# Attention units scaled one step behind their sums, products two units ahead, and more modulation chunks among them

## The chip, the cores and the metric

The kernel runs on one core of a Trainium2 chip. The metric is the device time of one execution in microseconds, as the median of several runs. A core has five engines with instruction streams of their own: TensorE (PE, with its weight loads as PEld), VectorE (DVE), ScalarE (ACT), GpSimd (POOL) and SyncE (SP), which here only issues DMAs. They are ordered by semaphores alone.

## The reference, cut to what matters

One step of a small model with two layers. The first layer mixes 384 tokens (128 of a prompt, 256 of a grid, so three tiles of 128) by attention, the second by a Hyena operator (a long convolution by FFT). Each is followed by a mixture of 32 experts.

```
m = silu(c) @ ada_w[l] + ada_b[l]             # 6 x 1024 values per layer: shifts, scales, gates
h = rmsnorm(x) * (1 + sc1) + sh1
p = h @ w_in                                   # q latent, kv latent, rotary key, nq, nk, nv
q = rmsnorm(rmsnorm(q_lat) @ w_q_up)           # 8 MLA heads of 96
k, v = from rmsnorm(kv_lat) @ w_kv_up          # keys normalised, too
nq, nk = rmsnorm per head                      # 8 neighbourhood heads of 64
out = softmax(q k^T * s (+ bias, mask)) v @ w_out
x = x + g1 * out
x = x + g2 * moe(rmsnorm(x) * (1 + sc2) + sh2)
```

The product of `silu(c)` with `ada_w` is the modulation: per layer 1024 x 6144 weights, 24 MB. It depends on nothing but `c`, so it can be computed anywhere before its use.

## The kernel before

The program is written engine by engine, each with its order of work by hand. Signals (`sig(name)`) count events; `.by(ins, i)` sets event i, `.at(eng, i)` waits for it. `link` makes an engine wait for its own last instruction.

**Modulation chunks.** The modulation is cut into 24 chunks of 512 columns (2 MB each, `ada`, 72 matmul instructions). Four of layer 0 come first; the other 20 (`chunks`) are spread over the attention: chunk 0 and 1 at units 7 and 9 (`at_unit`), the rest at 18 of the 24 pairs (`at_pair`). VectorE copies each result (`ada_row`, line 964). SyncE writes finished rows to DRAM in groups (`store_mod`, line 1867) and reads back the first layer's gate, broadcast to all partitions (`load_gate`, line 1879), as soon as the rows of chunk 1 have landed: a wait on SyncE's queue.

**The ring.** Weights come into a ring of three slots. Item n lies in slot n % 3 and may be loaded when item n - 3 is used: items 0 to 3 are chunks, 4 to 7 the columns of `w_in` (latents, nq, nk, nv), 8 the two up projections ("up"), 9 to 28 the 20 chunks, 29 and 30 the output weights, later ones belong to the Hyena layer. SyncE issues them in this order, so one that waits holds all behind it. "up" is free after the last k product.

**Units.** There are 13 units (`units`): nq, nk and q for three tiles each, k for four (the fourth is the cached context). For a unit TensorE makes the product (`produce`), ScalarE squares it (`square_unit`, one buffer `sq`), VectorE sums the squares per head (line 1032, for k also 1035), GpSimd raises to the power -0.5 (`unit_power`, line 1723), VectorE scales by that, by the gain, and rotates q and k of tiles 1 and 2 (line 952 is the helper of all these), TensorE turns the unit (`turn_unit`, lines 542, 544) and ScalarE copies it out. TensorE's loop makes the product of unit n+1, then a chunk if there is one, then turns unit n. The three nv products and the turned latents (`turn_latents`) stand before the product of unit 6. Scaled units lie in two buffers, and each accumulation takes the next of eight PSUM banks in turn (`open_`).

**Pairs.** Then 24 pairs of heads (12 MLA, 12 neighbourhood; the first four of each dozen have one block of 128 keys, the other eight three). For pair i TensorE makes the scores, turns the probabilities of pair i-2, multiplies those of pair i-3 with the values, and does a chunk if there is one, in bank 7. VectorE takes the maximum (line 1092), ScalarE the exponential (line 1540).

**Masks.** The bias of the neighbourhood heads is loaded (line 1914) after the "up" weights and masked on GpSimd (lines 1797, 1800) between the powers of units 5 and 6.

Of the kernel before, what the change touches and what calls it, by code (L numbers as in the profile page):

```python
# [171 lines left out]
def build(nc, a, stage=99):  # L172
    ctx = ExitStack()
    with ctx:
# [73 lines left out]

        def item(n, *dims):
            return v(RING + (n % 3) * MSLOT, *dims)  # L250
# [40 lines left out]
        for n, k in enumerate(items):  # L291
            loads[n % 3] += 16 * ndma.get(k[0], 1)
            landed[k] = loads[n % 3]
# [51 lines left out]
        at_unit = {7: chunks[0], 9: chunks[1]}  # L345
        at_pair = {int(1.32 * n) + 1: c for n, c in enumerate(chunks[2:])}
# [57 lines left out]
        w3_slot = RING + (number[("w3",)] % 3) * MSLOT  # L404
        W3, skip_row = v(w3_slot, 2 * D), v(w3_slot + 2 * D, 2 * D)
        nrow = [v(RING + (number["hyout", g] % 3) * MSLOT + 4096, 512) for g in range(2)]
# [18 lines left out]
        def _(pe):  # L425
# [3 lines left out]
            def arrived(k):  # L429
                pe.wait_ge(item_loaded[number[k] % 3], landed[k])  # L430
                return number[k]
# [5 lines left out]
            def ada(l, n, bank=None):  # L437
                i = arrived(("ada", l, n))
                w = item(i, KC, 512)
                brow = v(RING + (i % 3) * MSLOT + 4096, 512)  # L440
# [51 lines left out]
            def attention():  # L492
# [3 lines left out]
                for t in range(T):  # L496
                    hT_ready(0, t)
                    for kind, c0, c1 in (("qlat", 0, QR), ("kvr", QR, WIN0)):
                        o = open_(pe, kind, t, [("lat", t)])
# [4 lines left out]
                def produce(kind, t):  # L504
                    if kind in ("nq", "nk", "nv"):
                        w = item(arrived(("win", {"nq": 1, "nk": 2, "nv": 3}[kind])), KC, 512)
                        i = proj[kind, t, 0]
                        o = open_(pe, "proj", i, [("nv", t)] if kind == "nv" else [("normed", units.index((kind, t)))])
# [4 lines left out]
                    base = RING + (arrived(("up",)) % 3) * MSLOT  # L513
                    wq, wkv = v(base, 3, NH * QK), v(base + 2304, NH * 2 * NOPE)
                    sig("latT").at(pe, t)
                    for j in range(2):
                        i = proj[kind, t, j]
                        n = units.index((kind, t))
                        if kind == "q":
                            o = open_(pe, "proj", i, [("normed", n)])  # L520
                            for c in range(3):
                                last = mm(o[:, 0:384], LT[:, c, t * P:(t + 1) * P], wq[:, c, j * 384:(j + 1) * 384], c == 0, c == 2)
                        else:
                            o = open_(pe, "proj", i, [("normed", n), ("vout", t)])
# [3 lines left out]
                def turn_unit(kind, t):  # L528
# [18 lines left out]
                def turn_latents(t):  # L547
                    o = open_(pe, "latT", t, [("latT", t)])
# [399 lines left out]
        def _(dve):  # L948
# [67 lines left out]
            def attention():  # L1016
# [7 lines left out]
                for n, (kind, t) in enumerate(units):  # L1024
                    if n - 1 in at_unit:
                        l, c = at_unit[n - 1]
                        ada_row((l, c))
                    b = n % 2

                    sig("sq").at(dve, n)  # L1030
                    w = NOPE if kind != "q" else QK
# [4 lines left out]
                    sig("hms").by(red, n)  # L1036
                    sig("hrs").at(dve, n)
# [41 lines left out]
                    sig("normed").by(ins, n)  # L1079

# [345 lines left out]
        def _(act):  # L1426
# [35 lines left out]
            def attention():  # L1462
# [46 lines left out]
                square_unit(0)  # L1509
                for n, (kind, t) in enumerate(units):  # L1510
                    if n + 1 < len(units):
                        if units[n + 1] == ("q", 0):
# [7 lines left out]
                        square_unit(n + 1)  # L1520
# [196 lines left out]
        def _(pool):  # L1717
# [38 lines left out]
            def hyena():  # L1756
                for b in range(4):
# [4 lines left out]
                    if b == 0:  # L1762
                        pool.wait_ge(item_loaded[number[("w3",)] % 3], landed[("w3",)])
# [14 lines left out]
            if stage >= 1:  # L1778
# [15 lines left out]
                for hf in range(2):  # L1794
                    b = bias[64 * hf:64 * hf + 64].rearrange("p a b c d -> p (a b c) d")

                    link(pool.affine_select(out=b[:, :, 0:48], in_=b[:, :, 0:48], compare_op=ALU.is_ge, fill=NEG,
                                            base=8, pattern=[[0, 64], [1, 48]], channel_multiplier=-1))

                    sig("bias").by(pool.affine_select(out=b[:, :, 16:64], in_=b[:, :, 16:64], compare_op=ALU.is_ge, fill=NEG,  # L1800
                                                      base=-9, pattern=[[0, 64], [-1, 48]], channel_multiplier=1), hf)
                    sig("bias").at(pool, hf)
                for n in range(6, len(units)):
                    unit_power(n)
# [12 lines left out]
        def _(sp):  # L1817
            def load(k):
                n = number[k]
                if n >= 3:  # L1820
                    wait_used(sp, items[n - 3])
                s = item_loaded[n % 3]
                if k[0] == "ada":
                    _, l, c = k
                    sp.dma_start(item(n, KC, 512), a["ada_w"][l].rearrange("(p k) n -> p k n", k=KC)[:, :, c * 512:(c + 1) * 512]).then_inc(s, 16)  # L1825
                    o = RING + (n % 3) * MSLOT + 4096
# [4 lines left out]
                elif k[0] == "up":  # L1831
                    sp.dma_start(item(n, 3, NH * QK), a["mla_w_q_up"][0].rearrange("(c p) n -> p c n", p=P)).then_inc(s, 16)
                    sp.dma_start(v(RING + (n % 3) * MSLOT + 2304, NH * 2 * NOPE), a["mla_w_kv_up"][0]).then_inc(s, 16)
# [99 lines left out]
            if stage >= 3:  # L1933
# [9 lines left out]
                for k in items1[:3]:  # L1943
                    o = number[k] % 3 * MSLOT
# [74 lines left out]
```

## Time and profile before

| | us |
|---|---|
| median of 3 runs | 1339.37 (1339.36 to 1351.76) |
| the profiled execution | 1351.24 |
| its span | 1349.5 |
| TensorE busy | 1215.2 (90%) |
| VectorE, ScalarE, GpSimd busy | 589.8, 267.6, 201.0 |
| attention's units (from the first product of nq to the first scores) | 73.5 to 191 |
| attention's 24 pairs | 191 to 308.2 |

The span is from the first to the last instruction; the execution takes 1.7 us more. A busy share is an average over stages of different kinds. The chain that ended last lies 84% on TensorE and 5% on VectorE.

### The profile page before, as it was taken

The numbers are of one execution on the slowest core, as the hardware profiler recorded it, in microseconds if no ns is written. First come the engines' busy times: TensorE is split into PE (matmuls) and PEld (weight loads), VectorE is DVE, ScalarE is ACT, GpSimd is POOL, SyncE is SP. The second block draws the span as 40 slices with busy tenths as digits, with TensorE's granted clock in tenths as the row PEclk, the third lists the DMA queues.
The fourth block names the chain that finished last, engine by engine and source line by source line (L and its number), as shares of the span: only waits on it lengthen the run. The fifth ranks groups of instructions, "written<-read, shape, count | busy, mean of one in ns | idle before, by whom it ended". The sixth has DMA issues, their size and how long they took to land.

```text
span 1349.5 us, 26273 instructions
## 1 busy us (share of the span) xinstructions
PE 1215.2 (90%) x9235; PEld 704.2 (52%) x9236; DVE 589.8 (44%) x1223; ACT 267.6 (20%) x648; POOL 201.0 (15%) x249
## 2 busy tenths in 40 slices
PE   4799868989878899999979999999986899999996
PEld 3554545664545455555555654344554555555553
DVE  0122443462342344444554334777455144445445
ACT  1111332440201112112132113111010111211211
POOL 1025210000101122222200001111010022221231
PEclk9899977999778899999989999899985989999998
DMA  9533159993530989999952222000135089996894
GB/s 318 210 128 119 63 195 358 347 369 112 231 143 28 417 340 422 379 393 396 379 189 80 108 77 80 0 1 0 75 141 243 0 348 412 383 378 262 321 422 168
DMA packets 80143, 304.77 MB, mean 226 GB/s; under 512 B 10872, under 2 KB 11809, under 8 KB 54729
## 3 DMA queue, kind: packets, MB, share of 16 engines
q1 hardware_dynamic: 77098, 298.66, 57.0%
q10 hardware_dynamic: 2752, 4.53, 0.9%
q8 instruction: 51, 0.84, 0.3%
q0 software_dynamic: 224, 0.61, 0.1%
q14 instruction: 18, 0.15, 0.0%
HBM read 301.52 MB, written 2.24 MB: 225 GB/s over the span
## 4 chain that ended last, share of the span: by engine, by line
PE 84%; DVE 5%; DMA 4%; issue 2%; SPq 2%; ACT 1%; POOL 0%; POOLq 0%; DVEq 0%; ACTq 0%
PE banks L427 82%; DMA arena<-in_ada_b 3%; DVE arena L952 3%; SPq L1827 1%; PE banks L594 1%; DMA mod_rows<-arena 1%; PE banks L478 1%; SPq L1825 0%; PE banks L793 0%; DVE arena L998 0%; POOL arena L1723 0%; PE banks L542 0%; DVE arena L1092 0%; ACT arena L1459 0%; ACT arena L1550 0%
## 5 line engine op out<-in xcount | busy, mean ns | idle before, releaser
L427 PE MATMUL banks<-arena 32*128 32x256 f32 (+11 forms) x8904 | 1172.7, 424 | 88.8 <-DVE arena L952 15.6
L427 PEld LDWEIGHTS banks<-arena 128*32 128x32 f32 (+4 forms) x8904 | 662.5, 156 | 572.0 <-issue 406.5
L952 DVE TENSOR_TENSOR arena<-banks,arena 128x64 f32<-128x64 f32 (+4 forms) x284 | 113.9, 413 | 109.0 <-PE banks L427 74.5
L952 DVE TENSOR_TENSOR arena<-arena 128x384 f32<-128x384 f32 (+11 forms) x229 | 153.7, 677 | 4.9 <-PE banks L427 0.5
L1210 DVE SCALAR_TENSOR_TENSOR arena<-arena 128x768 f32<-128x768 f32 x81 | 82.9, 1024 | 92.3 <-issue 88.1
L1748 POOL COPY arena<-arena 128x256 f32 x79 | 65.0, 823 | 288.4 <-PE banks L427 154.9
L1584 ACT ACTIVATE arena<-banks 128x512 f32<-128x512 f32 x79 | 47.2, 597 | 250.8 <-PE banks L427 250.8
L1220 DVE TENSOR_SCALAR arena<-arena 128x64 f32<-128x64 f32 x79 | 15.4, 195 | 180.3 <-ACT arena L1588 180.3
L1739 POOL TENSOR_TENSOR arena<-arena 128x256 f32<-128x256 f32 x81 | 59.7, 737 | 225.3 <-PE banks L427 225.3
L1722 POOL TENSOR_SCALAR arena<-arena 128x8 f32<-128x8 f32 (+2 forms) x28 | 10.3, 369 | 379.2 <-ACT arena L1443 264.5
L1309 DVE TENSOR_SCALAR arena<-arena 128x385 f32<-128x385 f32 x24 | 11.6, 481 | 82.4 <-ACT arena L1645 82.4
L1222 DVE RECIPROCAL arena<-arena 128x64 f32<-128x64 f32 x79 | 43.7, 553 | 2.7
L1588 ACT ACTIVATE arena<-banks 128x64 f32<-128x64 f32 x79 | 17.7, 224 | 126.9 <-PE banks L427 126.9
L964 DVE COPY arena<-banks 128x128 f32<-128x128 f32 x24 | 7.0, 292 | 72.2 <-PE banks L427 72.2
L1580 ACT ACTIVATE arena<-banks 128x256 f32<-128x256 f32 x79 | 30.3, 384 | 41.3 <-PE banks L427 41.3
L1540 ACT ACTIVATE arena<-banks,arena 128x384 f32<-128x384 f32 (+1 forms) x48 | 24.0, 506 | 70.4 <-DVE arena L1093 61.3
L1443 ACT ACTIVATE arena<-arena 128x1024 f32<-128x1024 f32 x12 | 12.7, 1057 | 120.9 <-DVE arena L952 111.6
L1760 POOL TENSOR_TENSOR arena<-arena 128x512 f32<-128x512 f32 x4 | 5.1, 1263 | 209.2 <-DVE arena L952 209.2
L1723 POOL TENSOR_TENSOR arena<-arena 128x8 f32<-128x8 f32 (+2 forms) x28 | 30.5, 1090 | 2.3
L1644 ACT ACTIVATE arena<-banks,arena 128x128 f32<-128x128 f32 x24 | 8.8, 369 | 100.3 <-PE banks L427 100.3
L1195 DVE COPY arena<-banks 128x256 f32<-128x256 f32 x16 | 6.8, 425 | 48.2 <-PE banks L427 48.2
L1032 DVE TENSOR_REDUCE arena<-arena 128x8 f32<-128x512 f32 (+1 forms) x13 | 9.7, 744 | 38.4 <-ACT arena L1486 19.5
(144 smaller groups left out, 441.4 us busy)
## 6 DMA issues: line engine op xcount, KB each, us to landing
arena<-in_moe_w_gate SPq DMA_DIRECT2D x64, 1024.0 KB, 7.7
arena<-in_moe_w_up SPq DMA_DIRECT2D x64, 1024.0 KB, 9.8
arena<-in_moe_w_down SPq DMA_DIRECT2D x64, 1024.0 KB, 9.9
arena<-in_ada_w SPq DMA_DIRECT2D x24, 2048.0 KB
arena<-in_hy_w_in SPq DMA_DIRECT2D x6, 2048.0 KB
arena<-in_attn_w_in SPq DMA_DIRECT2D x3, 2048.0 KB
arena<-mod_rows SPq DMA_DIRECT2D x8, 512.0 KB, 8.8
arena<-in_attn_w_out SPq DMA_DIRECT2D x2, 2048.0 KB
```

The source lines that it names most:

```text
L427: return pe.matmul(out, lhsT, rhs, start=start, stop=stop, skip_group_check=True)
L952: return dve.tensor_tensor(o, p, q, op)
L1210: return dve.scalar_tensor_tensor(parts, posr, first_row[:, bass.ds(c, 1)], wr, ALU.is_equal, ALU.mult)
L1220: dve.tensor_scalar(e1, ex, 1.0, None, ALU.add).then_inc(s_["moe_dve"], 1)
L1222: dve.reciprocal(e2, e1).then_inc(s_["moe_dve"], 1)
L1540: ins = act.activation(PB[i % 2][:, r, 0:n, :].rearrange("p b k -> p (b k)"), ps[:, 2 * (i % 2) + r, 0:n * P], ACT.Exp, bias=negmax[:, c:c ...
L1580: act.activation(ysb, py, ACT.Copy).then_inc(s_["moe_y"], 1)
L1584: act.activation(gsb.rearrange("p i q f -> p (i q f)"), pg, ACT.Copy).then_inc(s_["moe_g"], 1)
L1588: act.activation(ex, pt[:, 0:2 * M].rearrange("p (f m) -> p f m", f=2), ACT.Exp, scale=-1.0).then_inc(s_["moe_e"], 1)
L1723: sig(name).by(pool.tensor_tensor(dst, dst, half_[:, 0:n], ALU.pow), i)
L1739: return pool.tensor_tensor(*two, bc(ones, 2), ALU.mult)
L1748: pool.tensor_copy(xcur, XS[:, :, bass.ds(first, M)]).then_inc(s_["moe_x"], 1)
```

## The change

Six edits, all around the attention:

- The ring: items 9 to 14 (chunks 0 to 5) use slots 0 and 1 in turn, and slot 2 stays with "up" until item 15. An item may be loaded when the last earlier item of its slot is used.
- Seven chunks (0 to 6) now go with units 6 to 12, the other 13 with pairs 1, 2, 4, 6, 8, 10, 12, 14, 16, 18, 20, 21 and 23.
- TensorE and ScalarE make products and squares two units ahead.
- VectorE sums the squares of unit n+1 before it scales unit n.
- PSUM banks of this phase are fixed: products in banks 0 to 5, turns in 6 and 7, chunks in 7.
- The bias is loaded before items 7 and 8, and masked on GpSimd behind the powers of units 1 and 3.

```diff
+        def place_of(n):
+            return n % 3 if n < 9 else (n - 9) % 2 if n < 15 else (n + 2) % 3
...
-        at_unit = {7: chunks[0], 9: chunks[1]}
-        at_pair = {int(1.32 * n) + 1: c for n, c in enumerate(chunks[2:])}
+        at_unit = {6 + n: c for n, c in enumerate(chunks[:7])}
+        at_pair = {int(1.9 * n) + 1: c for n, c in enumerate(chunks[7:])}
...
-                            o = open_(pe, "proj", i, [("normed", n)])
+                            o = open_(pe, "proj", i, [("normed", n)], n % 3 * 2 + j)
...
-                        o = open_(pe, "uT", i, [("uT", i)])
+                        o = open_(pe, "uT", i, [("uT", i)], 6 + j)
...
-                produce("nq", 0)
+                produce(*units[0])
+                produce(*units[1])
                 for n, (kind, t) in enumerate(units):
-                    if n + 1 < len(units):
-                        if units[n + 1] == ("q", 0):
+                    if n + 2 < len(units):
+                        if units[n + 2] == ("q", 0):
...
-                        produce(*units[n + 1])
+                        produce(*units[n + 2])
                     if n in at_unit:
-                        ada(*at_unit[n])
+                        ada(*at_unit[n], 7)
                     turn_unit(kind, t)
...
+                mean_squares(0)
+                for n, (kind, t) in enumerate(units):
+                    if n + 1 < len(units):
+                        mean_squares(n + 1)
+                    if n - 1 in at_unit:
+                        ada_row(at_unit[n - 1])
+                    b = n % 2
                     sig("hrs").at(dve, n)
...
                 square_unit(0)
+                square_unit(1)
...
-                        square_unit(n + 1)
+                        square_unit(n + 2)
                     turned(kind, t)
...
-                for n in range(6):
+                for n in range(len(units)):
                     unit_power(n)
-                pool.wait_ge(in_bias, 16)
+                    if n in (1, 3):
+                        hf = n // 2
+                        pool.wait_ge(in_bias, 16)
...
-                if n >= 3:
-                    wait_used(sp, items[n - 3])
+                held = [m for m in range(n) if place_of(m) == place_of(n)]
+                if held:
+                    wait_used(sp, items[held[-1]])
...
                 load(items0[6])
+                sp.dma_start(bias.rearrange("p a b c d -> p (a b c d)"), a["bias"]).then_inc(in_bias, 16)
                 load(items0[7])
                 load(items0[8])
-                sp.dma_start(bias.rearrange("p a b c d -> p (a b c d)"), a["bias"]).then_inc(in_bias, 16)
```

## Rows read from the trace of the kernel before

**Rows 1.** Busy time by stretch: each engine, granted clock, DMA share, GB/s.

```profile
73.50:137.00 63.50, 63.50 (x165) 29.05 (x164) 15.85 (x21) 8.15 (x21) 25.43 (x18) 1.00 0.36 131
137.00:191.00 54.00, 37.75 (x273) 24.14 (x271) 25.70 (x54) 19.58 (x43) 13.27 (x14) 0.86 0.28 100
191.00:308.20 117.20, 103.48 (x1732) 74.54 (x1733) 51.07 (x147) 44.21 (x144) 0.00 (x0) 0.90 0.96 345
```

**Rows 2.** Timeline of the q and k units: start, length, engine, line.

```profile
138.25 4.08 PE L427 MATMUL banks<-arena 128*128 128x384 f32 x12
...
148.09 1.08 PE L542 MATMUL banks<-arena 128*96 128x128 f32 x8 [1.45 <-DVE arena L952]
...
155.55 0.94 DVE L1032 TENSOR_REDUCE arena<-arena 128x8 f32<-128x768 f32 x1
156.12 1.88 PE L427 MATMUL banks<-arena 128*128 128x512 f32 x4
...
157.34 1.65 POOL L1723 TENSOR_TENSOR arena<-arena 128x8 f32<-128x8 f32 x1
...
159.03 1.02 DVE L952 TENSOR_TENSOR arena<-banks,arena 128x384 f32<-128x384 f32 x2 [2.54 <-POOL arena L1723]
160.09 2.28 DVE L952 TENSOR_TENSOR arena<-arena 128x768 f32<-128x768 f32 x5
...
162.42 1.94 PE L542 MATMUL banks<-arena 128*96 128x128 f32 x8 [4.42 <-DVE arena L952]
```

**Rows 3.** Timeline of SyncE's queue, 137 to 196 us.

```profile
137.03 0.55 SPq L1825 DMA_DIRECT2D arena<-in_ada_w  x1
...
180.48 0.55 SPq L1825 DMA_DIRECT2D arena<-in_ada_w  x1
...
184.43 1.38 SPq L1867 DMA_DIRECT2D mod_rows<-arena  x4
194.55 0.82 SPq L1879 DMA_DIRECT2D arena<-mod_rows  x2
195.41 0.55 SPq L1825 DMA_DIRECT2D arena<-in_ada_w  x1
```

**Rows 4.** Waits of SyncE's queue: us in total, times, longest.

```profile
SPq L1879 <- DMA mod_rows<-arena: 8.7, 1, 8.7
```

**Rows 5.** Busy time by stretch, as rows 1.

```profile
144.00:146.00 2.00, 2.00 (x8) 1.21 (x7) 0.00 (x0) 0.49 (x1) 1.89 (x2) 1.00 0.24 93
...
201.00:208.00 7.00, 0.39 (x8) 0.15 (x12) 0.92 (x5) 1.25 (x6) 0.00 (x0) 0.67 1.04 386
```

**Rows 6.** Timeline of VectorE's maxima: pairs 0, 4, 7, 9, 11, 19, 21, 23.

```profile
192.27 0.42 DVE L1092 TENSOR_REDUCE arena<-banks 128x2 f32<-128x256 f32 x1 [4.80 <-PE banks L427]
...
215.05 0.96 DVE L1092 TENSOR_REDUCE arena<-banks 128x2 f32<-128x768 f32 x1 [2.54 <-PE banks L427]
...
228.14 0.96 DVE L1092 TENSOR_REDUCE arena<-banks 128x2 f32<-128x768 f32 x1 [1.17 <-PE banks L427]
...
238.77 0.96 DVE L1092 TENSOR_REDUCE arena<-banks 128x2 f32<-128x768 f32 x1 [1.17 <-PE banks L427]
...
247.46 0.96 DVE L1092 TENSOR_REDUCE arena<-banks 128x2 f32<-128x768 f32 x1 [1.17 <-PE banks L427]
...
281.60 0.96 DVE L1092 TENSOR_REDUCE arena<-banks 128x2 f32<-128x768 f32 x1
...
290.99 0.96 DVE L1092 TENSOR_REDUCE arena<-banks 128x2 f32<-128x768 f32 x1
...
299.78 0.96 DVE L1092 TENSOR_REDUCE arena<-banks 128x2 f32<-128x768 f32 x1
```

**Rows 7.** Timeline of GpSimd: the first of the four mask instructions.

```profile
119.68 3.22 POOL L1797 TENSOR_SCALAR_AFFINE_SELECT arena<-arena 64x3072 f32<-64x3072 f32 x1 [0.16 <-POOL arena L1723]
```

**Rows 8.** Timeline of TensorE: a chunk at full clock and at half.

```profile
26.84 2.31 PE L427 MATMUL banks<-arena 128*32 128x128 f32 x72 [0.64 <-DMA arena<-in_ada_b]
...
35.50 4.21 PE L427 MATMUL banks<-arena 128*32 128x128 f32 x72 [5.48 <-DMA arena<-in_ada_b]
```

More of the change, by code:

```diff
@@ L291, in build @@
         for n, k in enumerate(items):
-            loads[n % 3] += 16 * ndma.get(k[0], 1)
-            landed[k] = loads[n % 3]
+            loads[place_of(n)] += 16 * ndma.get(k[0], 1)
+            landed[k] = loads[place_of(n)]
         item_loaded = [sem(f"item_loaded{i}") for i in range(3)]
@@ L403, in build @@
         f3 = v(MODO + 1536, NTOK)
-        w3_slot = RING + (number[("w3",)] % 3) * MSLOT
+        w3_slot = ring(number[("w3",)])
         W3, skip_row = v(w3_slot, 2 * D), v(w3_slot + 2 * D, 2 * D)
-        nrow = [v(RING + (number["hyout", g] % 3) * MSLOT + 4096, 512) for g in range(2)]
+        nrow = [v(ring(number["hyout", g]) + 4096, 512) for g in range(2)]
         trow = [v(w3_slot + 4 * D, 512), nrow[1]]
@@ L429, in arrived @@
             def arrived(k):
-                pe.wait_ge(item_loaded[number[k] % 3], landed[k])
+                pe.wait_ge(item_loaded[place_of(number[k])], landed[k])
                 return number[k]
@@ L507, in produce @@
                         i = proj[kind, t, 0]
-                        o = open_(pe, "proj", i, [("nv", t)] if kind == "nv" else [("normed", units.index((kind, t)))])
+                        if kind == "nv":
+                            o = open_(pe, "proj", i, [("nv", t)], 2 * t + 1)
+                        else:
+                            n = units.index((kind, t))
+                            o = open_(pe, "proj", i, [("normed", n)], n % 3 * 2)
                         for k in range(KC):
@@ L1023, in attention, with mean_squares @@
                     sig("lat").by(dve.tensor_copy(lat[:, t, QR + KVR:WIN0], kv[:, KVR:KVR + ROPE]), t)
[L1024 to L1028, printed above, removed]
+                def mean_squares(n):
+                    kind, t = units[n]
                     sig("sq").at(dve, n)
-                    w = NOPE if kind != "q" else QK
+                    b, w = n % 2, NOPE if kind != "q" else QK
                     red = dve.tensor_reduce(hms[:, b, :], sq[:, 0:NH * w].rearrange("p (h w) -> p h w", h=NH), AX, ALU.add)
@@ L1079, in attention @@
                     sig("normed").by(ins, n)
+                ada_row(at_unit[len(units) - 1])
                 for i in range(NU + 1):
@@ L1509, in attention @@
                 square_unit(0)
+                square_unit(1)
                 for n, (kind, t) in enumerate(units):
-                    if n + 1 < len(units):
-                        if units[n + 1] == ("q", 0):
+                    if n + 2 < len(units):
+                        if units[n + 2] == ("q", 0):
                             for tt_ in range(T):
@@ L1762, in hyena @@
                     if b == 0:
-                        pool.wait_ge(item_loaded[number[("w3",)] % 3], landed[("w3",)])
+                        pool.wait_ge(item_loaded[place_of(number[("w3",)])], landed[("w3",)])
                     for g in range(2):
@@ L1789, in unit_power @@
                     power(hrs[:, n % 2, :], hms[:, n % 2, :], 8, "hrs", n)
-                for n in range(6):
+                for n in range(len(units)):
                     unit_power(n)
-                pool.wait_ge(in_bias, 16)
[L1794 to L1804, printed above, removed]
+                    if n in (1, 3):
+                        hf = n // 2
+                        pool.wait_ge(in_bias, 16)
+                        b = bias[64 * hf:64 * hf + 64].rearrange("p a b c d -> p (a b c) d")
+                        link(pool.affine_select(out=b[:, :, 0:48], in_=b[:, :, 0:48], compare_op=ALU.is_ge, fill=NEG,
+                                                base=8, pattern=[[0, 64], [1, 48]], channel_multiplier=-1))
+                        sig("bias").by(pool.affine_select(out=b[:, :, 16:64], in_=b[:, :, 16:64], compare_op=ALU.is_ge, fill=NEG,
+                                                          base=-9, pattern=[[0, 64], [-1, 48]], channel_multiplier=1), hf)
+                        sig("bias").at(pool, hf)
             if stage >= 2:
```

22 lines of the change are left out of this document (12 added, 10 removed).

## The prediction

> **What bounds the kernel now.** I read the busy time by stretch first [rows 1]. From 73.5 to 137.0 us (products nq, nk, nv) TensorE is busy without a gap; from 137 to 191 us (turns and scaling of the q and k units) it is busy 37.8 of 54.0 us while the DMA engines carry 100 GB/s; from 191 to 308.2 us (24 pairs of heads, 18 chunks) the DMA engines are 96% busy and TensorE 88%. So the first stretch is bound by TensorE, the middle one by something else, the last one by transfers or TensorE.
>
> For the middle stretch I read the timeline of one unit [rows 2]. The sum of squares of unit q2 starts at 155.55 on VectorE, GpSimd's power follows at 157.34, the scaling at 159.03 to 162.37, and only then does TensorE turn the unit (162.42). With one buffer of squares and the next sum queued behind the scaling, unit after unit walks sum, power, scaling, turn, with 2 us of GpSimd in the middle.
>
> For the last stretch I read SyncE's queue [rows 3, 4]. Chunk 1 is issued at 137.03, chunk 2 only at 180.48: its slot is held by the "up" weights until the last k product, and everything later waits behind it. From 180.48 on chunks come back to back. After the fourth one the queue stands still until the rows of the modulation have landed (8.7 us), then the gate (1 MB) goes out at 194.55. The pairs read it off in VectorE's maximum of each pair [rows 6]: pair 0 at 192.27, pair 4 at 215.05, because the chunk issued at 195.41 let TensorE start again only at 207.9 (it was busy 0.39 of 7.0 us before, at a granted clock of 0.67 [rows 5]). From pair 4 on the time is TensorE's, not DMA's: each pair costs more with a chunk than without.
>
> **The change, part by part.** Call the 20 chunks c0 to c19 and the pairs p0 to p23. Before, c0 and c1 are in units, c2 to c19 in 18 pairs. After, c0 to c6 are in units 6 to 12, c7 to c19 in pairs 1, 2, 4, 6, 8, 10, 12, 14, 16, 18, 20, 21, 23. No work is removed; 5 chunks move from pairs to units.
>
> *Masks and bias.* The four mask instructions cost GpSimd some 3.2 us each [rows 7]. Moved behind units 1 and 3, each two delay one power by 6.5 us; a unit there lasts about 7 us of TensorE and the products run two ahead, so about 7 us of cover stand over it. Its DMA (2 MB) now goes between the loads of nk and nv. SyncE waits there for the slot of nv anyway, until 73.5 us. Cost nothing; were the cover gone, at most 2 x 6.5 us. The fixed banks I also cost at nothing, with one exception: a chunk now sits in bank 7, where the second half of each q or k turn goes, so that half waits for VectorE's copy of the chunk row, some 0.3 us behind the chunk.
>
> *Units 6 to 12, as a schedule.* Prices, all [rows 2, 8]: q product 4.0, k product 1.8, chunk 2.3 at full clock, turn 1.1, scaling of a q unit with its sum 0.95 + 3.4 on VectorE. The latents are done at 138 as now. Then q0, q1, q2 and two nk turns: 151.0; c0: 153.3; turn q0, k0, c1: 158.5; turn, k1: 161.4. c2 may be loaded only from 153.3 (its slot is c0's). One chunk alone takes 7.5 us from issue (137.03 to about 144.5 [rows 3, 5]), so 160.8: no wait. c2 ends 163.7, turn and k2: 166.6. c3 was issued at 158.5, behind c2 by 5.4 us of transfer (2.1 MB at 386 GB/s [rows 5]): 166.3, no wait. c3 ends 168.9, turn and k3: 171.8. VectorE needs 4.35 + 0.3 of these 5.1 us a unit, with the power hidden, so it just keeps up.
>
> Now c4. Behind c3's issue the queue of SyncE holds store_mod, which waits for c1's row (158.8), four small stores, and load_gate, which waits until they have landed. What is queued behind that wait: c4, c5, c6, and TensorE waits for them. Before, the stores were issued at 184.43 and done 9 us later, when the two chunks ahead of them were through; by that they are done here about when c3 is, at 167. The gate goes at 167.2. Gate to first use of the chunk behind it took 194.55 to 207.94, 13.4 us, with a second chunk on its heels as here: c4 at 180.6. By bytes at 386 GB/s c5 comes at 183.5, c6 at 189.0. TensorE pauses from 171.8 to 180.6 and then runs at half clock for some 10 us, as it did from 208 to 217 (a chunk costs 4.2 there [rows 8]). So: c4 184.8, turn 187, c5 191.2, turn 192.7, c6 195, turn and ck 197; p0's maximum 198.3, against 192.27 before. The units get 6 us longer and hold 5 more chunks.
>
> On this wait the Trainium skill bears (DMA: Bandwidth & Descriptors, section Queues, rings and completion order): the increment of a DMA's semaphore lands only after every earlier write of that DMA engine. The trace agrees: the stores behind two chunks took 9 us. Were the small stores free of the chunk ahead, the gate could go at 162, which is the first rival below.
>
> *p0 to p4.* c7 is issued when c4 is used (184.8) and lands behind c6 at 195; c8 waits for c5's row (191.5) and 1.2 us of stores and lands at 201; c9 follows c6's use (195) and lands at 207. Pairs of one key block with a chunk took 3.1 us at full clock (p2 to p3). p1 199.2, p2 202.3, p3 205.4, p4 207.4. Before: 215.05. Here the half clock and the 6.6 us wait of rows 5 go; late next is c9, which p4's chunk just meets. Gain 7.6 us.
>
> *p4 to the end.* Two MLA pairs with two chunks take 10.63 us (228.14 to 238.77), with one 8.69 (to 247.46) [rows 6]: a chunk is worth 1.94. Two NA pairs: 9.39 (281.60 to 290.99) and 8.79 (to 299.78), so 0.60: there the pair without a chunk waits for its own softmax, and the chunk had filled that. p4 to p11 lose 2 chunks (3.9), p12 to p15 one (0 to 2.3, taken 2.3, since these short pairs are all TensorE), p16 to p23 one (0.6). Gain 6.8 us. A chunk is wanted every 8.3 us or more and brought every 5.4, so transfers no longer bind.
>
> *Sum.* 7.6 + 6.8 = 14.4 us earlier at 308.2. Everything behind waits for the last pair (the output product, then the experts' loads, which wait for the residual) and moves along. The other slots of the Hyena input weights change nothing: they landed before 693 and TensorE did not wait for them. Against the profiled execution: 1351.24 - 14.4 = 1336.8, of which the span is all but 1.7. The median of the runs before lies 11.9 under the profiled one, and I carry the difference over: 1339.4 - 14.4 = 1325.0.
>
> **Rivals.** (a) *The stores are quick, or TensorE's pause vanishes.* If they land 2 us after issue, the gate goes at 162 and c4 at 163.7. DMA then runs on from 153.3: eight chunks to c9 at 5.4 us, the gate at 4.5 and 1.5 of latency give 202.5 for p4's chunk, and p4 at 202.5 instead of 207.4. Gain 12.5 + 6.8 = 19.3: 1320. For it: before, the stores waited behind 4.2 MB, here behind half a chunk. Against: the gate's own slowness stays, and c3 is still ahead.
>
> (b) *Most of it is given back.* Pairs without a chunk leave gaps; after one of 2 us (p17, 274.9) TensorE fell to half clock and p18 took 2 us longer. Before there were 5 pairs without a chunk from p4 on, now 9. Two to four such falls, and c5 or c6 some 3 us later than I have them, leave 5 us: 1334. For it: the one fall in the trace. Against: four of the five gaps had none.
>
> (c) *Slower: the half clock stays.* After the pause at 171.8 TensorE gets 1.2 GHz and the looser pairs never bring it back. A pair of three key blocks without chunk costs TensorE at most (8.69 - 2.31) / 2 = 3.2 us; at half clock 2.3 more, a chunk 1.9 more [rows 8], on half the pairs: 3.3 us a pair. It decides from four and a half pairs beyond the schedule (14.4 / 3.3); over the 20 from p4 on, with the short ones at half price and what the waits for softmax absorb, about 40 us, so 1365. For it: the granted clock was 0.5 to 0.7 from 184 to 217. Against: from 217 on it came back and stayed at 0.97 in the mean, with TensorE busy 92%, and after the change some 90%.
>
> The Trainium skill has the cause behind (b) and (c) (TensorE: Matmul & The Clock Gate, What's actually happening): the array is throttled by default and activity releases it. Nothing in it says that the falls would be many here; by it alone my sum would not change.
>
> **Chances.** What a measurement of this kernel can tell from no change is about 1%, 13.4 us, so the line is 1326.0. My forecast (1325.0, its own range 1321 to 1330) 0.50, cut by the line nearly in half: 0.27 faster, 0.23 same. (a) 0.25, faster. (b) 0.15, same. (c) 0.10, of it 0.08 slower by over 1% and 0.02 within. Faster 0.52, same 0.40, slower 0.08. The range reaches from 1315 (a with a softer clock loss) to 1341: one of the three runs before was 12 us above the other two, and forecast or (b) in that level end there; it leaves out (c).
>
> **What would show it.** In the profile after: the first sum of unit n+1 before the scaling of unit n; chunk issues at about 153, 158, then a hole until 167; p0 at 198, p4 at 207, the last pair at 294. Wrong if the hole is missing (a), if the clock is below 0.9 in the mean behind 207 (b, c), if VectorE waits for a chunk row with TensorE idle beyond 1 us per unit, or if GpSimd's masks hold a turn before 137.

## The result and the profile after

| | before | after |
|---|---|---|
| median of the runs, us | 1339.39 (1339.36 to 1351.76, 4 runs) | 1331.49 (1330.41 to 1332.38, 4 runs) |
| ratio after / before, 95% interval | | 0.9888 (0.9845 to 0.9932) |
| the same pair measured again | 1346.17 (11 runs) | 1326.69 (6 runs), 0.9842 (0.9801 to 0.9883) |
| profiled execution: time, span | 1351.24, 1349.5 | 1331.81, 1330.0 |
| last pair done in the trace | 308.15 | 293.76 |

The change made the kernel faster, by 1.1% in the ratio. Forecast were 1325.0 and a range of 1315 to 1341. The medians alone differ by 7.9 us, 0.6%. The ratio is further from one. The run of before that was 12 us above the others explains a part of that (by means it is 1331.4 against 1342.5, 0.992); the rest can't be followed from the runs listed. Here and below, ratios leave out executions more than 1.5% above the fastest of their kernel, medians don't.

The end of the attention ("last pair") is read from SyncE's queue: it issues the read-back of the modulation rows (two DMAs) the moment the last pair is done. Busy time by stretch, as [rows 1], the first stretch from 73.0:

```profile
73.00:137.00 64.00, 64.00 (x173) 30.09 (x172) 13.56 (x19) 8.96 (x17) 25.18 (x17) 1.00 0.29 100
137.00:191.00 54.00, 43.35 (x579) 29.25 (x581) 27.78 (x60) 15.79 (x36) 13.29 (x14) 0.91 0.80 280
191.00:308.20 117.20, 104.30 (x1458) 70.37 (x1449) 54.25 (x151) 45.77 (x147) 0.00 (x0) 0.97 0.81 284
```

In the second stretch the DMA engines now carry 280 GB/s where it was 100, and TensorE does 5.6 us more. In the third, DMA is busy 81% instead of 96%.

One q unit and what follows, in the timeline (as [rows 2]; the helper line 952 is now 964, 1032 is 1040). The sum of the next unit comes at 149.04, the scaling of this one at 150.99:

```profile
149.04 0.95 DVE L1040 TENSOR_REDUCE arena<-arena 128x8 f32<-128x768 f32 x1 [1.44 <-ACT arena L1504]
150.16 0.24 POOL L1741 TENSOR_SCALAR arena<-arena 128x8 f32<-128x8 f32 x1 [2.32 <-DVE arena L1040]
150.48 1.66 POOL L1742 TENSOR_TENSOR arena<-arena 128x8 f32<-128x8 f32 x1
150.65 1.12 PE L553 MATMUL banks<-arena 128*96 128x128 f32 x8
...
150.78 0.29 DVE L976 COPY arena<-banks 128x128 f32<-128x128 f32 x1 [0.79 <-PE banks L434]
150.99 1.01 DVE L964 TENSOR_TENSOR arena<-banks,arena 128x384 f32<-128x384 f32 x2
```

The power of unit 8 runs while VectorE scales unit 7, and TensorE turns unit 6 at 150.65 with no wait. The copy of the chunk row (L976) stands between the two.

SyncE's queue (as [rows 3]) and TensorE over the same time:

```profile
150.78 0.55 SPq L1844 DMA_DIRECT2D arena<-in_ada_w  x1
...
155.79 0.55 SPq L1844 DMA_DIRECT2D arena<-in_ada_w  x1
...
156.93 1.15 SPq L1886 DMA_DIRECT2D mod_rows<-arena  x4
164.90 0.82 SPq L1898 DMA_DIRECT2D arena<-mod_rows  x2
165.77 0.55 SPq L1844 DMA_DIRECT2D arena<-in_ada_w  x1
```

```profile
159.51 2.31 PE L434 MATMUL banks<-arena 128*32 128x128 f32 x72 [1.01 <-DMA arena<-in_ada_b]
...
166.65 3.92 PE L434 MATMUL banks<-arena 128*32 128x128 f32 x72 [2.06 <-DMA arena<-in_ada_b]
...
171.47 1.88 PE L434 MATMUL banks<-arena 128*128 128x512 f32 x4
179.03 4.22 PE L434 MATMUL banks<-arena 128*32 128x128 f32 x72 [5.68 <-DMA arena<-in_ada_b]
...
185.44 2.30 PE L434 MATMUL banks<-arena 128*32 128x128 f32 x72 [0.82 <-ACT arena L1525]
```

Chunks 2 and 3 go out at 150.78 and 155.79, then the queue stands until 164.90. TensorE waits 1.0 us for chunk 2, 2.1 for chunk 3 and 5.7 for chunk 4; behind the last two of these waits a chunk takes 3.9 and 4.2 us instead of 2.3. At 185.44 it is back at full clock.

SyncE's wait for the stores (as [rows 4]):

```profile
SPq L1898 <- DMA mod_rows<-arena: 6.8, 1, 6.8
```

The trace's packet records say what this wait is. When the stores were issued (156.93), 1.6 of the 4.2 MB of chunks 2 and 3 had started to move, so 2.6 MB stood ahead of them. Their own packets, of 512 bytes, ran from 162.98 to 163.92, and the last store had landed at 164.89. So 6 us pass before they move, where chunk 2, with nothing ahead, moved 1.3 us after its issue, and 1 us passes behind their last packet. In before it is the same: issued at 184.43, packets from 192.99, landed at 194.53.

VectorE's maxima of pairs 0 and 4 (as [rows 6]):

```profile
195.59 0.43 DVE L1110 TENSOR_REDUCE arena<-banks 128x2 f32<-128x256 f32 x1 [3.05 <-PE banks L434]
...
207.81 0.96 DVE L1110 TENSOR_REDUCE arena<-banks 128x2 f32<-128x768 f32 x1 [0.87 <-PE banks L434]
```

The units end 3.3 us later than before (192.27), pair 4 comes 7.2 us earlier (215.05), the last pair 14.4 us earlier.

A part of it was made long before the units. TensorE's timeline between the last turned modulation row (L460) and the first product of the attention, in after:

```profile
44.75 0.43 PE L460 MATMUL banks<-arena 128*128 128x128 f32 x2 [0.51 <-DVE arena L976]
47.05 44.53 PE L434 MATMUL banks<-arena 128*128 128x384 f32 x144 [1.87 <-ACT arena L1471]
```

It is 2.30 us; in before (43.62 to 48.35) it is 4.73, and there TensorE waits for VectorE's last copy of the modulated tiles.

By the first product of a q unit (q0 below) after is 2.46 us ahead:

```profile
135.79 4.08 PE L434 MATMUL banks<-arena 128*128 128x384 f32 x12
```

In before it starts at 138.25 [rows 2]. The sum is: 2.43 from the shorter gap, 0.73 because the products behind it run less time at half clock (mean granted clock 0.83 in the first 10 us, against 0.74), 0.43 because one turn now comes behind q0, and 1.13 lost, since in after the last chunk before the gap ran at half clock (4.12 us against 2.31). That last one isn't the change's: in the second profile of before that chunk took 3.99 us, too.

### The profile page after: what moved, and what is told of

Read it like the earlier page. It is cut to its first block, busy times and chain, and to the rows that moved or that the text cites. A ratio compares the mean times of both kernels' runs of the same rounds, so it can differ in the third digit from the quotient of the medians.

```text
span 1330.0 us, 26274 instructions
## 1 busy us (share of the span) xinstructions
PE 1205.2 (91%) x9235; PEld 697.4 (52%) x9236; DVE 588.3 (44%) x1223; ACT 267.2 (20%) x648; POOL 200.9 (15%) x249
## 4 chain that ended last, share of the span: by engine, by line
PE 85%; DVE 5%; DMA 4%; issue 2%; ACT 2%; SPq 2%; POOLq 0%; POOL 0%; DVEq 0%; ACTq 0%
PE banks L434 83%; DMA arena<-in_ada_b 3%; DVE arena L964 3%; SPq L1846 1%; PE banks L606 1%; SPq L1844 1%; DVE arena L1110 1%; DMA mod_rows<-arena 1%; PE banks L485 1%; ACT arena L1569 1%; ACT arena L1559 1%; PE banks L805 0%; ACT arena L1477 0%; PE banks L555 0%; ACT arena L1461 0%
## 5 line engine op out<-in xcount | busy, mean ns | idle before, releaser
L964 DVE TENSOR_TENSOR arena<-arena 128x384 f32<-128x384 f32 (+11 forms) x229 | 153.3, 675 | 4.6 <-PE banks L434 0.2
L976 DVE COPY arena<-banks 128x128 f32<-128x128 f32 x24 | 7.0, 292 | 77.9 <-PE banks L434 77.9
```

Source lines behind the costliest of these rows:

```text
L964: return dve.tensor_tensor(o, p, q, op)
```

## The experiments

I judge the kernels by the end of the attention in their traces first, because what lies behind it varies by more than most of them differ (the controls, at the end). "Last pair" is always SyncE's issue behind it. The start differs, too: q0 comes between 132.6 and 139.5, partly by the gap above and partly by how the chunks before it happen to land. So the table also has the time from q0 to the last pair. It varies less: 157.97 and 157.84 in the two profiles of after, 169.90 and 171.11 in those of before.

| kernel | chunks in units / pairs | q0 | pair 0 | pair 4 | last pair | q0 to last pair | median us (runs), ratio to before |
|---|---|---|---|---|---|---|---|
| before | 2 / 18 | 138.25 | 192.27 | 215.05 | 308.15 | 169.90 | |
| before, second profile | 2 / 18 | 138.49 | 192.44 | 215.66 | 309.60 | 171.11 | 1353.03 (5), 1.0075 |
| after | 7 / 13 | 135.79 | 195.59 | 207.81 | 293.76 | 157.97 | 1331.49 (4), 0.9888 |
| after, second profile | 7 / 13 | 134.96 | 194.33 | 206.84 | 292.80 | 157.84 | 1326.69 (6), 0.9842 |
| e1 order alone | 2 / 18 | 133.41 | 175.07 | 196.76 | 288.34 | 154.93 | 1327.38 (9), 0.9881 |
| e2 chunks alone | 7 / 13 | 139.50 | 203.36 | 212.67 | 297.69 | 158.19 | 1336.12 (10), 0.9931 |
| e3 after, gate later | 7 / 13 | 135.46 | 190.96 | 201.30 | 287.12 | 151.66 | 1326.21 (4), 0.9878 |
| e4 after, masks late | 7 / 13 | 134.67 | 193.76 | 206.14 | 290.04 | 155.37 | 1323.83 (1) |
| e5 order, gate later | 2 / 18 | 134.22 | 175.88 | 189.63 | 287.26 | 153.04 | 1329.44 (6), 0.9883 |
| e6 gate later, five in units | 5 / 15 | 134.30 | 182.31 | 191.94 | 282.23 | 147.93 | 1327.14 (6), 0.9848 |
| e6 again | 5 / 15 | 134.24 | 182.31 | 192.97 | 283.17 | 148.93 | 1325.56 (6), 0.9823 |
| e7 before, gate later | 2 / 18 | 137.36 | 191.07 | 204.99 | 302.37 | 165.01 | 1333.52 (1) |
| e8 gate later, four in units | 4 / 16 | 135.60 | 181.17 | 198.15 | 288.47 | 152.87 | 1330.91 (10), 0.9858 |
| e9 after, sum not ahead | 7 / 13 | 132.60 | 197.12 | 207.35 | 292.88 | 160.28 | 1334.09 (1) |

Before, after and e6 have two profiles each, the others one. The ratios are each to runs of before measured beside them. Those of after, e1, e3, e5, e6 and e8 lie between 0.982 and 0.989 with intervals that overlap: the differences between their attentions are shown in the traces, not in the whole time.

Theory 1 is that of the prediction: the units were bound by the chain of sum, power and scaling; SyncE's wait for the stored rows holds chunk 4; from pair 4 on each chunk less is worth its price. Theory 2 is given with each.

**e1: the order alone.** From after:

```diff
-            return n % 3 if n < 9 else (n - 9) % 2 if n < 15 else (n + 2) % 3
+            return n % 3
...
-        at_unit = {6 + n: c for n, c in enumerate(chunks[:7])}
-        at_pair = {int(1.9 * n) + 1: c for n, c in enumerate(chunks[7:])}
+        at_unit = {7: chunks[0], 9: chunks[1]}
+        at_pair = {int(1.32 * n) + 1: c for n, c in enumerate(chunks[2:])}
...
-                ada_row(at_unit[len(units) - 1])
```

The fixed banks and the new place of the masks stay in, so it is the order with these two.

> After, but with the ring and the places of the chunks as before (2 in units, 18 in pairs). Theory 1 (sum, power and scaling in a chain bound the units; the order two ahead removes it): TensorE's work from 137 on is about 34 us, so the scores start near 172 instead of 191, chunk 2 is issued near 160 instead of 180.5, and the rest keeps its shape: last pair near 289, time 15 to 20 us under before, more than the whole change. Theory 2 (the chunks moved into units bring the gain, the order only makes room for them): the last pair no earlier than 300, time within 8 us of before.

The last pair stands at 288.34, 19.8 us before that of before and 5.4 before that of the whole change. SyncE's queue and the maxima of pairs 3 and 4:

```profile
163.06 0.55 SPq L1843 DMA_DIRECT2D arena<-in_ada_w  x1
...
167.48 1.15 SPq L1885 DMA_DIRECT2D mod_rows<-arena  x4
177.16 0.82 SPq L1897 DMA_DIRECT2D arena<-mod_rows  x2
178.03 0.55 SPq L1843 DMA_DIRECT2D arena<-in_ada_w  x1
```

```profile
182.75 0.42 DVE L1109 TENSOR_REDUCE arena<-banks 128x2 f32<-128x256 f32 x1 [0.32 <-PE banks L434]
196.76 0.96 DVE L1109 TENSOR_REDUCE arena<-banks 128x2 f32<-128x768 f32 x1 [1.17 <-PE banks L434]
```

The "up" weights are free 17.4 us earlier than in before (chunk 2 at 163.06 against 180.48), and the whole rest slides forward with its shape, the hole between the stores and chunk 4 included. Theory 1 holds: without the moved chunks the gain is there, and larger. From q0 on it is 15.0 us, against 11.9 for the whole change; the other 4.8 us of the 19.8 lie before q0, 2.4 of them in the gap of the banks. So the moved chunks, in the form that the change gives them, cost 3.0 us.

**e2: the chunks and the ring alone**, in before: the new `place_of`, `at_unit` and `at_pair`, one copy of a chunk row behind the last unit, no other edit.

> Before, with the new ring and 7 chunks in units 6 to 12, but products one unit ahead and the sum behind the scaling. Theory 1: each unit still takes 6.5 to 7 us and the up weights stay until the product of the last unit, so chunk 6 is issued near 184 and the scores start near 195; five fewer chunks in the pairs give 7 us, so the last pair is at 300 to 303, time 5 to 8 us under before. Theory 2: the last pair at 294 to 297, nearly all of the gain.

297.69, 10.5 us under before: between the two theories' numbers, nearer to theory 2's. (Only its attention is read; what lies behind it took 1048.4 us, the longest of all.) Here the gain comes from elsewhere than in e1: chunk 2 is issued at 150.18 instead of 180.48, and chunks fill TensorE's waits. The scores start 11 us later than in before (pair 0 at 203.36), since the last k product comes late and chunk 6 needs its slot; pair 4 is still 2.4 us earlier, and from there on 85.0 us against 93.1 are 8.1 less for five chunks fewer, 1.6 of it because TensorE's clock didn't fall at pair 18 here (see e4). But q0 came 1.25 us later than in before. From q0 on the gain is 11.7 us, 10.1 without the clock's part, against 11.9 for the whole change: nearly all of it, as theory 2 had it. So from q0 on the parts give 15.0 and 11.7 us alone and 11.9 together: they are two ways to fill the same idle time, and don't add.

**e3: the gate later.** From after, and the same edit in e5 to e8:

```diff
                 for k in items0[9:]:
                     load(k)
+                    if k == ("ada",) + chunks[12]:
+                        load_gate(0, 0)
...
-                        if items[n][1:] == (0, 5):
-                            load_gate(0, 0)
```

> After, but the first layer's gate is read back only behind the load of chunk 12, so SyncE does not wait for the stores of rows ahead of chunk 4. Theory 1 (this wait holds chunk 4, and with it TensorE's pause of 6 us and the half clock behind it): chunk 4 is issued near 161 and used near 173, scores start 5 to 7 us earlier, last pair at 287 to 290, time 4 to 7 us under after. Theory 2 (bandwidth with two slots sets the units' pace, the wait only hides it): pause moves to chunks 5 and 6, last pair within 2 us of 293.8.

```profile
156.60 1.15 SPq L1886 DMA_DIRECT2D mod_rows<-arena  x4
161.67 0.55 SPq L1844 DMA_DIRECT2D arena<-in_ada_w  x1
```

```profile
171.95 2.31 PE L434 MATMUL banks<-arena 128*32 128x128 f32 x72 [0.55 <-DMA arena<-in_ada_b]
...
178.91 4.22 PE L434 MATMUL banks<-arena 128*32 128x128 f32 x72 [3.61 <-DMA arena<-in_ada_b]
```

Chunk 4 is issued at 161.67, 4.1 us earlier, and used at 171.95 instead of 179.03. A wait of 3.6 us appears in front of chunk 5, as theory 2 had it, but the last pair is at 287.12, 6.6 us under after. The wait of SyncE held chunk 4; behind it transfers are nearly as late. The edit does two things: it takes away the wait (4.1 us at the issue of chunk 4), and it takes the gate's 1 MB from ahead of chunk 4, which now needs 10.3 us from issue to use instead of 13.3. No run has one without the other.

**e7: the same edit in before.**

> Before, with only the gate's read-back moved behind the load of chunk 12. The same wait stood in front of chunk 4 there (8.7 us). Theory 1: chunk 4 goes out at 186 instead of 195.4, TensorE's wait before pair 4 shrinks by 5 to 7 us, pair 4 at 208 to 210 instead of 215, last pair at 301 to 303. Theory 2: with 18 chunks in the pairs bandwidth takes it back later, last pair at 305 or later.

Pair 4 at 204.99 and the last pair at 302.37, 5.8 us under before and at theory 1's number. The hold was there all along; it isn't the change's doing. Pair 4 comes 10.1 us earlier, more than at the last pair: at pair 15 TensorE waits 3.8 us for a chunk, as in e5 below.

**e5: the order alone and the gate later.**

> Order alone (as e1), and the gate read back only behind the load of chunk 12. In e1 chunk 4 was issued at 178.03 though its slot had been free since the units; it waited for the stores. Theory 1 (the wait is what costs): chunk 4 goes out near 169, TensorE's wait of 8.0 us before pair 4 goes almost whole, pair 4's maximum near 187 instead of 196.8, last pair near 280. Theory 2 (transfers alone set the pace from 163 on): three chunks and then one each 5.4 us, chunk 5 lands no earlier than now less the gate's 4 us, last pair at 284 to 285. Time 4 to 8 us under e1.

Pair 4 comes at 189.63, 7.1 us before that of e1, near theory 1. The last pair at 287.26 is only 1.1 us before. Between them TensorE waits 3.7 us for chunk 13:

```profile
241.44 5.52 PE L434 MATMUL banks<-arena 128*32 128x128 f32 x76 [3.68 <-DMA arena<-in_ada_b]
```

This chunk was issued at 225.98, right behind the gate's read-back (223.44), and used 15.5 us later. In e7 it was the same (issued 241.30 behind the gate at 238.77, used 15.6 us later). With 18 chunks in the pairs and the gate's megabyte among them, transfers take back what pair 4 had gained: neither theory said that. A place for the gate where no chunk is due soon was not tried.

**e6: five chunks in units.** After with the gate later and

```diff
-        at_unit = {6 + n: c for n, c in enumerate(chunks[:7])}
-        at_pair = {int(1.9 * n) + 1: c for n, c in enumerate(chunks[7:])}
+        at_unit = dict(zip((6, 7, 8, 10, 12), chunks[:5]))
+        at_pair = {int(1.6 * n) + 1: c for n, c in enumerate(chunks[5:])}
```

> After with the gate later (as e3) and 5 chunks in units (6, 7, 8, 10, 12), 15 in pairs. Theory 1 (the two slots left beside the up weights deliver a chunk per load and use, so seven in a row make TensorE wait): with gaps between them the waits for chunks in the units fall from 9 us to under 4, scores start near 183, pair 4 near 193, and with two chunks more in the pairs (4 us) the last pair at 281 to 284. Theory 2 (bandwidth from 150 on sets the end of the units however many are in them): last pair within 2 us of e3's 287.1.

TensorE's waits for chunks from 137 us on fall to 2.3 us (after: 11.9, e3: 9.0), pair 0 stands at 182.31, the last pair at 282.23: theory 1, and the earliest attention of all, 10.6 us under the second profile of after (9.9 from q0 on). It was run again:

> e6 once more, unchanged. Its last pair stood 10.6 us before that of after, but its time (1327.1) no lower than after's on that chip (1326.7). Theory 1: the attention's end repeats (282 +- 1) and what lies behind it varies by chance, so in more runs the time comes out some 10 us under after's, near 0.977 of before. Theory 2: a shorter attention puts the experts or Hyena into a worse phase of TensorE's clock each time, and the ratio to before stays near 0.985.

The attention's end repeats (283.17), the time doesn't follow: 0.9823 (0.9784 to 0.9862) of before, against 0.9842 (0.9801 to 0.9883) for after. The intervals overlap nearly whole. So e6 has the shorter attention, shown twice, but that its execution is shorter than after's is not shown.

**e8: four in units** (6, 8, 10, 12; the other 16 at every 1.5 pairs).

> As e6 with 4 chunks in units (6, 8, 10, 12) and 16 in pairs. If TensorE's work in the units still bounds there (each chunk 2.3 us) and a chunk in the MLA pairs costs 1.9, in the NA pairs 0.6, moving one more chunk into the pairs is worth 0.4 to 1.7 us: last pair at 280.5 to 282. Rival: transfers bind in the pairs from 16 chunks on as they did with 18 in e5, last pair at 284 or later.

288.47, the rival: between the maxima of pairs 2 and 3 (184.49 and 194.24) TensorE waits 4.2 us for a chunk, and pair 4 is 5 to 6 us later than in e6. Of the splits tried, five in units is the one with least waiting on both sides.

**e9: the sum not ahead.**

```diff
-                mean_squares(0)
                 for n, (kind, t) in enumerate(units):
-                    if n + 1 < len(units):
-                        mean_squares(n + 1)
                     if n - 1 in at_unit:
                         ada_row(at_unit[n - 1])
+                    mean_squares(n)
```

> After, but VectorE sums the squares of unit n only after it has scaled unit n-1, as before; products and squares stay two ahead. Theory 1 (the sum one ahead takes the power out of the chain): each q or k unit costs sum 0.95, power 2.4 and scaling up to 3.4 in a row, 6.5 to 7 us against 5 to 6, so the units are slower, the wait for chunk 4 is partly covered, scores start 3 to 6 us later than after's (pair 0 at 198 to 200) and the last pair is at 296 to 299. Theory 2 (it is the products two ahead that matter, which free the up weights early): last pair within 1 us of 293.

The last pair at 292.88 is that of after (293.76, 292.80), theory 2's number. But q0 started 3.2 and 2.4 us earlier than in the two profiles of after:

```profile
132.60 4.08 PE L434 MATMUL banks<-arena 128*128 128x384 f32 x12
```

So from q0 on e9 takes 160.3 us against 158.0 and 157.8. Its head start is gone by the end, and the sum one ahead is worth 2.3 to 2.4 us, by one profile. In the timeline the chain is back, power at 155.81, scaling at 157.50:

```profile
155.81 1.66 POOL L1740 TENSOR_TENSOR arena<-arena 128x8 f32<-128x8 f32 x1
...
157.50 1.02 DVE L964 TENSOR_TENSOR arena<-banks,arena 128x384 f32<-128x384 f32 x2 [2.17 <-POOL arena L1740]
```

but chunks fill TensorE's time behind it, and the waits for chunks shrink from 11.9 to 6.1 us in exchange. From the use of chunk 4 to pair 0 e9 takes 21.7 us (175.44 to 197.12), after 16.6 (179.03 to 195.59); 2.0 of that difference of 5.1 us come back by pair 4, on the way to which after waits for a chunk. The products two ahead were never taken out alone, so what they carry isn't shown. Nor was the sum tried in e1 or e6, where transfers hold the units less.

**e4: the masks late.**

> After, with the bias loaded behind the up weights and both masks behind the power of unit 5, as before. Prediction's step: the masks cost nothing in either place. There they stand ahead of the power of q0; that is made from 141.5 on, and the masks end near 132, so the last pair stays at 293.8 +- 1. Rival: the bias load pushes the first chunk or the masks hold unit 6, and the last pair comes 3 us or more later.

290.04, 2.8 and 3.7 us earlier than the two profiles of after, and not the same, as I expected, nor later. Most of it isn't the masks': at pair 18 TensorE fell to half clock in both profiles of after (mean granted clock 0.76 over that pair) and not here (1.00). From that pair's maximum to the next it is 5.27 us here, 6.89 there:

```profile
259.08 0.96 DVE L1110 TENSOR_REDUCE arena<-banks 128x2 f32<-128x768 f32 x1
264.35 0.96 DVE L1110 TENSOR_REDUCE arena<-banks 128x2 f32<-128x768 f32 x1
```

Another 0.3 to 1.1 us lie before q0, and 0.4 between pairs 16 and 17. What is left is 0.4 to 0.6 us between q0 and pair 4, and one profile can't tell that from chance. In after TensorE is busy 64.0 of 64.0 us up to 137, so the masks in their new place opened no gap there.

**The controls, and what lies behind the attention.**

> The kernel before, unchanged, to see what an execution at its usual 1339 us looks like beside the profiled one of 1351.24. If the 12 us sit in TensorE's clock, some stretch behind the attention (the turns before the first experts, or the first dozen expert steps) is shorter here by several us at a higher granted clock, and the attention still ends at 308 +- 1. Rival: the attention itself ends 5 us or more earlier in the usual execution, so that the attention's gain of the change is smaller than 14.4 us there.

> After, unchanged, on the same chip as the others. The last pair at 293.8 +- 1 again; what lies behind it differs from the other profile by up to 7 us with the granted clock, as between the two profiles of before.

The attention's end repeats within 1.5 us: 308.15 and 309.60, 293.76 and 292.80. Not so the rest. From the last pair to the end of the span:

| | first experts | Hyena | second experts | all |
|---|---|---|---|---|
| before | 254.9 | 308.2 | 275.0 | 1041.4 |
| before, second | 249.6 | 313.0 | 277.8 | 1039.2 |
| after | 251.8 | 307.1 | 274.9 | 1036.2 |
| after, second | 254.4 | 308.4 | 277.7 | 1042.4 |
| e4 | 247.0 | 308.0 | 275.1 | 1032.0 |
| e7 | 251.3 | 306.0 | 271.8 | 1029.3 |
| e6, first and second | 250.3, 258.7 | 312.9, 307.9 | 277.9, 273.5 | 1041.8, 1043.4 |

(The columns are from the first expert step to the first sum of squares behind it, from there to the next such, and from the first step of the second experts to the end; the stretches between them are left out.) The work there is the same in all of these kernels (only the ring slots of some weights differ), and the sums differ by 14 us. Identical kernels differ by 6 us (after), and by 8.4 us in one part of them (e6). The granted clock over the span goes with it: 1350.63 to 1355.51 us at 0.926 to 0.931 in the five runs of the control of before, 1336.73 us at 0.937 in a run of the same kernel beside it. This control has a ratio of 1.0075 (1.0045 to 1.0105) to itself, so an interval of this kind is too narrow by that much. The 0.9888 and 0.9842 of after lie beyond that, on the other side of one.

My expectation for the control of before failed in part: the attention ended at 309.6, as theory 1 had it, but this execution was again one of the long ones, so that where the usual execution saves its 12 us was never seen in a profile.

## Why the prediction was right, and where it was off

- *What bounds.* Right for the units with two chunks: in e1 they end 17.2 us earlier, 12.4 of it behind q0. Of the two halves that I named, the power in the chain is worth some 2.4 us with seven chunks (e9); the product one ahead was not tried by itself. With seven chunks the order adds little, since TensorE waits for transfers: from q0 on e2 takes 158.2 us, or 159.8 with the fall of the clock that after has, and after 158.0.
- *Fixed banks at nothing.* This step failed, in the change's favour: they shorten a gap by 2.4 us. In before the first product of the attention is the sixteenth accumulation, so the turning count gives it bank 7, which holds the last tile's transposes, copied out last by VectorE; its new bank 0 has been free for long. The gap is 4.72 to 4.73 us in the four traces without fixed banks (both of before, e2, e7) and 2.29 to 2.30 in both of after and in e1; in e4, e5, e6 and e9 it is 2.6 to 3.2, because there TensorE waits for `w_in` to land. No run changes the banks alone, but no other edit touches what runs there. The cost that I did name, a turn held by the copy of the chunk row, is 0.04 us in after (1.12 against 1.08) and shows once in e1, with 0.41.
- *Masks at nothing.* No gap before 137 in after; e4 leaves 0.4 to 0.6 us open.
- *The schedule of units 6 to 12.* Chunk 2 issued at 150.8 (forecast 153.3), chunk 3 at 155.8 (158.5), gate at 164.9 (167.2), chunk 4 used at 179.0 (180.6), pair 0 at 195.6 (198.3). All some 2.5 us early, as q0 is; the hole at the stores was where I put it, and e3 shows that the gate's read-back makes it. The waits of 1.0 and 2.1 us that I called none come from chunks used 8.7 and 10.9 us after issue, not 7.5 and 7.8. Half clock behind the pause lasted 6.4 us, not 10.
- *p0 to p4.* Pair 4 at 207.8 (forecast 207.4, 7.6 us; measured 7.2). Right, because the transfers set this point: chunk 8 was forecast to land at 201 and its product starts at 201.20. Pair 0 came 2.7 us before its forecast, so TensorE waited 2.1 us there and ran that chunk at half clock (4.5 us), which I had not.
- *p4 to the end*, 6.8 us: 86.0 us against 93.1, 7.1. Right; e2 and e3 have 85.0 and 85.8, e1 with its 18 chunks 91.6.
- *The sum*: 14.4 us at the last pair, measured 14.4, and 15.6 from the means of two profiles each (308.9 and 293.3). That it fits to a tenth is luck: 2.5 of the 14.4 us lie before q0, where I had nothing, and from q0 on it is 11.9 (13.3 between the second profiles).
- *Carried over to the median*: here it was off. The span fell by 19.5 us, the medians beside it by 7.9, those of the second measurement by 19.5. I carried the 14.4 from one profiled execution to a median and gave the 12 us between two executions of before only to the range. The term that was missing is what varies behind the attention: 6.2 us between the two profiles of after, as large as the distance from the forecast to the result (6.5 us). That this is what made the 6.5 us isn't shown, since no profile caught an execution of before at 1339.4.
- *Rivals.* (a), quick stores, didn't happen by itself; e3, which takes the wait and the gate's transfer away, gave 6.6 us, where I had 4.9 between it and the forecast. Its argument had the amount wrong: not half a chunk stood ahead of the stores but 2.6 MB, more than one. (b), more falls of the clock: one fall, at p18, as before. I wrote that it cost 2 us there; the traces without the fall (e2, e4, e5) have 5.27 us from pair 18 to 19 where before has 6.84, so it is 1.6. (c), a lasting half clock: no; from 207 to the last pair the mean granted clock was 0.98. The 2.3 us that I added to a pair at half clock follow from no row that I named.
- The page of the Trainium skill named for the stores (DMA: Bandwidth & Descriptors, section Queues, rings and completion order) says that a semaphore's increment lands only after every earlier write of its DMA engine. The trace doesn't contradict it, but that isn't what made this wait: the stores' own packets started only 6 us after issue, when the chunk ahead had all but moved, and landed about 1 us after the last of them.
- *Transfers no longer bind from p4 on*: holds with 13 chunks in the pairs (85.0 to 86.0 us from pair 4 to the last; 83.9 in e4); with 18 and the gate among them (e5, e7) TensorE waits again, and a wait stands at pair 3 with 16 (e8).

What stays open: whether the time behind the attention depends on when the attention ends. e6's two medians lie 1044.9 and 1042.4 us above the end of its attention, after's 1037.7 and 1033.9, and the runs don't tell that from chance.

## What to carry to other kernels

When two edits fill the same idle time, price each alone: from q0 to the last pair the order was worth 15 us, the chunks 12, both 12, and the best mix (five chunks, gate later) 21 to 22. Look in a DMA queue for an item that waits for its own stores; what matters is what stands behind it, and moving such a read-back with its megabyte behind a few loads gave 5.8 us in one kernel and 6.6 in another, and 1.1 in a third, where it then held a chunk that was due. Look also at the bank that a new phase opens first. And compare kernels between two marks inside the trace when the stretches before and behind them vary by more than the change is worth: by the last mark alone the sum one ahead seemed worth nothing (e9), between two it was 2.4 us.

## What the runs showed of the hardware that was not expected

TensorE went to half clock behind a wait of 2.06 us (chunk 3, 3.92 us instead of 2.31) and kept full clock behind one of 1.01 us and, in e3, behind one of 1.94. The length of the wait alone doesn't decide it: behind the same wait of 2.04 us at pair 18 it fell in after and not in e4. Small stores queued behind 2.6 and 3.4 MB of loads started to move only 6.0 and 8.6 us after their issue, though each is 2 KB. The same work behind the attention took 1029 to 1044 us in the profiles other than e2's, the first experts alone between 247 and 259.
